# Output projection of a two-block transformer kernel: the first four row tiles accumulated together over weight chunks

## The reference

```
first block:   h = rms_norm(x) * (1 + scale) + shift          (scale, shift, gate from silu(c) @ w_ada)
               q, k, v, gates = split(h @ w_in)
               oa = forgetting_attention(...) * silu(za);  ob = sliding_window_attention(...) * silu(zb)
               y  = concat(oa, ob) @ w_out                    # 2048 x 1024 times 1024 x 1024
               x  = x + gate * rms_norm(y)
second block:  16 meta tokens ahead; a = sparse latent attention * silu(gate_a)
               r  = rms_norm(hgrn2(...)) * silu(gate_h)
               y  = concat(a, r) @ w_out
               out = layer_norm(2**0.25 * h + y) * ln_g + ln_b
```

## Time and profile before

| | |
|---|---|
| median of three runs | 3832.46 us |
| the profiled execution | 3833.1 us, span 3831.4 us |
| TensorE busy, granted clock | 3363.4 us (88%), 0.936 of 2.4 GHz |
| VectorE, ScalarE, GpSimd busy | 2068.3, 1388.9, 894.7 us |
| output stage one, first and last matmul | 1522.72 and 1699.21 us |
| output stage two, first matmul and last result | 3639.14 and 3828.25 us |
| matmuls of L850, each of three kinds | x512, 396, 393 and 393 ns mean |

### The profile page before, as it was taken

The page is one execution under the profiler, slowest core; times in us unless marked ns, Lnnn a source line. Parts: engine busy times, 40 slices in busy tenths (PEclk is TensorE's granted clock), DMA queues, the critical chain, the costliest instruction groups (busy, mean ns, idle before and its releaser), DMA issues. The chain is left out here.

```text
span 3831.4 us, 44650 instructions
## 1 busy us (share of the span) xinstructions
PE 3363.4 (88%) x15906; PEld 2532.0 (66%) x15906; DVE 2068.3 (54%) x3915; ACT 1388.9 (36%) x2368; POOL 894.7 (23%) x815
## 2 busy tenths in 40 slices
PE   6898999699999996986699989795996989999698
PEld 3688888566656664875577768584774656666387
DVE  4200101366666665331489999995674544545466
ACT  3100001034444444221258888122553333333344
POOL 0120111156454461001322222242231021111100
PEclk9899999889999998998899999897997999999899
DMA  6221223456554423444211353245135354444454
GB/s 220 63 76 51 77 76 117 125 123 130 119 122 109 106 71 109 132 148 164 71 47 54 91 182 90 84 144 172 56 116 166 104 134 122 118 112 113 129 159 130
DMA packets 386851, 433.92 MB, mean 113 GB/s; under 512 B 113046, under 2 KB 302838, under 8 KB 374824
## 3 DMA queue, kind: packets, MB, share of 16 engines
q1 hardware_dynamic: 276044, 306.45, 28.6%
q10 hardware_dynamic: 104000, 86.95, 7.8%
q0 software_dynamic: 6592, 37.75, 3.5%
HBM read 298.41 MB, written 132.62 MB: 113 GB/s over the span
## 5 line engine op out<-in xcount | busy, mean ns | idle before, releaser
L2179 PE MATMUL f_pO<-f_PT,f_vv 128*128 128x512 f32 (+3 forms) x944 | 379.3, 484 | 25.0 <-ACT f_PT L2208 25.0
L2266 DVE CUSTOM_DVE_ANT_0 n_junk<-n_pM,n_chosen 128x512 bf16<-128x512 f32 (+4 forms) x352 | 200.8, 572 | 305.1 <-PE n_pM L2100 150.4
L2261 DVE TENSOR_REDUCE f_mxc<-f_pM 128x1 f32<-128x512 f32 (+2 forms) x448 | 240.0, 540 | 222.3 <-PE f_pM L2104 127.9
L2575 PE MATMUL cbank<-hT_high,cw_hi 128*128 128x512 f32 x800 | 321.4, 402 | 35.9 <-POOL kpartsI L2547 15.9
L2754 DVE TENSOR_SCALAR_CACHE_REDUCE sharedI<-xI,TI 128x384 bf16<-128x384 f32 (+8 forms) x284 | 349.0, 1294 | 0.1
L590 PE MATMUL p_bank<-hT_high,p_w_hi 128*128 128x512 f32 (+1 forms) x768 | 306.7, 399 | 43.6 <-POOL p_w_lo L556 38.6
L2208 ACT ACTIVATE f_PT<-f_pS 128x512 f32<-128x512 f32 (+3 forms) x472 | 221.2, 473 | 334.3 <-PE f_pS L2143 165.8
L2208 ACT ACTIVATE n_PT<-n_pS 128x512 f32<-128x512 f32 (+4 forms) x352 | 177.6, 504 | 424.3 <-PE n_pS L2158 424.1
L2575 PE MATMUL cbank<-hT_high,cw_lo 128*128 128x512 f32 x800 | 316.0, 395 | 0.0
L2575 PE MATMUL cbank<-hT_low,cw_hi 128*128 128x512 f32 x800 | 315.4, 394 | 0.0
L2179 PE MATMUL n_pO<-n_PT,n_vv 128*128 128x512 f32 (+4 forms) x704 | 312.8, 526 | 0.0
(11 more groups left out here) (408 smaller groups left out, 7387.6 us busy)
## 6 DMA issues: line engine op xcount, KB each, us to landing
n_mkt<-scratch_mask_turned ACTq DMA_DIRECT2D x256, 128.0 KB, 2.1
cw_raw<-in_w_in_dram SPq DMA_DIRECT2D x50, 512.0 KB, 4.6
f_zz<-scratch_z SPq DMA_DIRECT2D x128, 128.0 KB, 3.0
p_w_raw<-in_w_in_dram SPq DMA_DIRECT2D x23, 512.0 KB, 3.9
wa<-in_w_ada_dram SPq DMA_DIRECT2D x8, 1024.0 KB, 5.8
xt<-in_x_dram SPq DMA_DIRECT2D x16, 512.0 KB, 6.8
scratch_z<-p_stage ACTq DMA_DIRECT2D x32, 256.0 KB, 2.4
scratch_qk_high<-p_stage ACTq DMA_DIRECT2D x32, 256.0 KB, 2.5
```

What stands on the lines that cost most here:

```text
L2179: pe.matmul(pO[:, B % 2, c0:c1], lhsT=vv[0:nk, b, kt, :], rhs=PT[0:nk, u % PR, c0:c1], start=(kt == 0 and not heads[h].local), stop=(heads ...
L2261: v.tensor_reduce(to, pM[:, n % 2, 0:wd], AX.X, ALU.max).then_inc(s_mx, 1)
L2266: v.tensor_tensor_reduce(junk[:, n % 2, 0:wd], pM[:, n % 2, 0:wd], chosen[:, at:at + wd], 1.0, 3.0 * NEG, ALU.add, ALU.max, accum_out=to). ...
L2575: last = pe.matmul(bank[:, p % RING, 0:wd], lhsT=w_part[pw][b][:, c, :], rhs=rhs, start=(c == 0 and a == 0), stop=(c == DC - 1 and a == 2))
```

## The change

In both output stages the first FIRST = 4 row tiles are multiplied together: for weight chunk k, TensorE does all 6 matmuls of each of the four tiles, then goes to chunk k+1. pY gets four buffers (eight banks), G_hi and G_lo four each. Tiles 4 to 15 are multiplied as before. The weights come in eight DMAs of 512 KB. The engines' order is written out anew in `in_order`, and SP's order in the loops after `load`. gT, og, zg, xg and tt keep two buffers. One more wait stands in VectorE's gate (s_lo).

```
-        AHEAD, BEHIND = 3, 1
-        def skeleton(phases): ...
+        FIRST = 4
+
+        def in_order(gate, split, finish, weight):
+            for n in range(FIRST):
+                for g in ((0, 1) if n == 0 else (n + 1,)):
+                    gate(g)
+                split(n)
+                weight(n)
+            for k in range(FIRST, DC):
+                weight(k)
+            for n in range(FIRST, NT + 2):
+                if n < NT:
+                    split(n)
+                if n + 1 < NT:
+                    gate(n + 1)
+                for t in {FIRST: (0, 1), FIRST + 1: (2, 3)}.get(n, (n - 2,)):
+                    finish(t)
```

On SP (the waits within load_parts, load_turned, load_rows and store are as before):

```
-            parts = ((3, load_parts),) if part is not None else ()
-            skeleton(parts + ((2, load_turned), (-1, store), (1, load_rows)))
+            def load(n):
+                if part is not None:
+                    load_parts(n)
+                load_turned(n)
+            for n in range(2):
+                load(n)
+            for n in range(2):
+                load_rows(n)
+            for n in range(2, 6):
+                load(n)
+            for n in range(NT):
+                store(n)
+                if n + 2 < NT:
+                    load_rows(n + 2)
+                for t in {0: (), 1: (6,), 2: (), 3: (7,)}.get(n, (n + 4,)):
+                    if t < NT:
+                        load(t)
```

On TensorE:

```
-                pe.wait_ge(s_lo, n + 1)
-                pe.wait_ge(s_res[b], r)
-            for z in range(2):
-                pe.wait_ge(s_wl[z], DC // 2)
-            skeleton(((0, multiply),))
+            for k in range(DC):
+                pe.wait_ge(s_wl[k % 2], k // 2 + 1)
+                for n in range(FIRST):
+                    if k == 0:
+                        pe.wait_ge(s_lo, n + 1)
+                    for z in range(2):
+                        last = products(n, k, z)
+                    if k == DC - 1:
+                        last.then_inc(s_y, 1)
+            for n in range(FIRST, NT):
+                pe.wait_ge(s_lo, n + 1)
+                pe.wait_ge(s_res[n % 2], n // 2 - 1)
+                for z in range(2):
+                    for k in range(DC):
+                        last = products(n, k, z)
+                last.then_inc(s_y, 1)
```

`products(n, k, z)` is the three passes of tile n, chunk k, half z, into pY[:, n % 4]. On GpSimd, ScalarE and VectorE:

```
-            for k in range(0, DC, 2):
-                gp.dma_start(wraw[:, k:k + 2, :], ...).then_inc(s_w[k // 2], 16)
-            split_low(gp, 1)
+            for k in range(DC):
+                gp.dma_start(wraw[:, k, :], w_out[0, k * P:(k + 1) * P, :]).then_inc(s_w[k], 16)
+            for k in range(1, DC, 2):
+                weight_low(gp, k)
...
-            skeleton(((1, high), (-1, finish)) + (((2, gate),) if part is not None else ()))
+            in_order(gate, high, finish, weight)          # ScalarE
...
                 if n >= 2:
                     v.wait_ge(s_hi, n - 1)
+                    v.wait_ge(s_lo, n - 1)
...
-                if n >= 2:
-                    v.wait_ge(s_y, n - 1)
+                if n >= 4:
+                    v.wait_ge(s_y, n - 3)
...
-            skeleton(((1, low), (-1, finish)) + (((2, gate),) if part is not None else ()))
+            in_order(gate, low, finish, weight)           # VectorE
```

More of the change, by code:

```diff
@@ L757, in stage_out @@
             sig = m.sb(n_("sig"), [P, HW])
-        G_hi = [m.sb(n_(f"Ghi{i}"), [P, DC, P], F32R) for i in range(2)]
-        G_lo = [m.sb(n_(f"Glo{i}"), [P, DC, P], F32R) for i in range(2)]
+        G_hi = [m.sb(n_(f"Ghi{i}"), [P, DC, P], F32R) for i in range(4)]
+        G_lo = [m.sb(n_(f"Glo{i}"), [P, DC, P], F32R) for i in range(4)]
         junk = m.sb(n_("junk"), [P, D])
@@ L764, in stage_out @@
             gain, offset = m.sb(n_("gain"), [P, D]), m.sb(n_("offset"), [P, D])
-        pY = m.ps(n_("pY"), [P, 2, D])
-        s_w = [m.sem(n_(f"w_loaded{i}")) for i in range(DC // 2)]
+        pY = m.ps(n_("pY"), [P, 4, D])
+        s_w = [m.sem(n_(f"w_loaded{i}")) for i in range(DC)]
         s_wh, s_wl = m.sem(n_("w_high")), [m.sem(n_(f"w_low{i}")) for i in range(2)]
@@ L814, in load_turned, with load_rows, store @@
                 sp.dma_start(gT[:, b], gated_T.rearrange("(k p) t -> p k t", p=P)[:, :, ds(n * P, P)]).then_inc(s_gt[b], 16)
-            def load_rows(n, b, r):
+            def load_rows(n):
+                b, r = n % 2, n // 2
                 sp.wait_ge(s_res[b], r)
                 sp.dma_start(xg[:, b, :], rows_in[ds(n * P, P), :]).then_inc(s_x[b], 16)
-            def store(n, b, r):
+            def store(n):
+                b, r = n % 2, n // 2
                 sp.wait_ge(s_res[b], r + 1)
@@ L825, in _, with weight_low @@
+            for n in range(NT):
[5 more added lines that the diff above has]
+                        load(t)
             for b in range(2):
                 sp.wait_ge(s_st[b], 8 * NT)
[L828 to L833, removed]
+        def weight_low(eng, k):
+            eng.wait_ge(s_wh, k + 1)
+            eng.tensor_tensor(w_lo[:, k, :], wraw[:, k, :], w_hi[:, k, :].bitcast(F32), ALU.subtract
+                              ).then_inc(s_wl[k % 2], 1)
@@ L843, in _, with products @@
         def _(pe):
-            def multiply(n, b, r):
+            def products(n, k, z):
+                for a, (pg, pw) in enumerate(PASSES):
+                    last = pe.matmul(pY[:, n % 4, z * HW:(z + 1) * HW], lhsT=(G_hi, G_lo)[pg][n % 4][:, k, :],
+                                     rhs=(w_hi, w_lo)[pw][:, k, z * HW:(z + 1) * HW],
+                                     start=(k == 0 and a == 0), stop=(k == DC - 1 and a == 2))
+                return last
+            for k in range(DC):
[7 more added lines that the diff above has]
+                        last.then_inc(s_y, 1)
@@ L853, in multiply, with weight, gate @@
                 last.then_inc(s_y, 1)
-            for z in range(2):
-                pe.wait_ge(s_wl[z], DC // 2)
-            skeleton(((0, multiply),))
         @block.scalar
         def _(act):
-            for k in range(DC):
-                act.wait_ge(s_w[k // 2], 16)
+            def weight(k):
+                act.wait_ge(s_w[k], 16)
                 act.activation(w_hi[:, k, :], wraw[:, k, :], ACT.Copy).then_inc(s_wh, 1)
-            def gate(n, b, r):
+            def gate(n):
+                if part is None:
+                    return
+                b, r = n % 2, n // 2
@@ L867, in gate, with high, finish @@
                 act.activation(sig[:], zg[:, b, :], ACT.Sigmoid).then_inc(s_sig, 1)
-            def high(n, b, r):
+            def high(n):
+                b, r, c = n % 2, n // 2, n % 4
                 act.wait_ge(s_gt[b], r * 16 + 16)
-                if n >= 2:
-                    act.wait_ge(s_y, n - 1)
-                last = act.activation(G_hi[b][:, 0:GIVEN], gT[:, b], ACT.Copy)
+                if n >= 4:
+                    act.wait_ge(s_y, n - 3)
+                last = act.activation(G_hi[c][:, 0:GIVEN], gT[:, b], ACT.Copy)
                 if part is not None:
                     act.wait_ge(s_gated, n + 1)
-                    last = act.activation(G_hi[b][:, GIVEN:].rearrange("p a b -> p (a b)"), g1[:, b, :], ACT.Copy)
+                    last = act.activation(G_hi[c][:, GIVEN:].rearrange("p a b -> p (a b)"), g1[:, b, :], ACT.Copy)
                 last.then_inc(s_hi, 1)
-            def finish(n, b, r):
+            def finish(n):
+                b = n % 2
                 if ln:
@@ L893, in _, with weight, gate @@
             own_ = Tally(v, s_dve)
-            split_low(v, 0)
-            def gate(n, b, r):
+            def weight(k):
+                if k % 2 == 0:
+                    weight_low(v, k)
+            def gate(n):
+                if part is None:
+                    return
+                b, r = n % 2, n // 2
                 v.wait_ge(s_in[b], r * 32 + 32)
@@ L941, in finish @@
                 else:
-                    own_.up(v.scalar_tensor_tensor(tt[:, b, :], pY[:, b, :], rstd[:, one], gate_row[:],
+                    own_.up(v.scalar_tensor_tensor(tt[:, b, :], pY[:, n % 4, :], rstd[:, one], gate_row[:],
                                                    ALU.mult, ALU.mult))
```

33 lines of the change are left out of this document (14 added, 19 removed).

## The result

| | before | after |
|---|---|---|
| median of six runs | 3832.74 us | 3901.55 us (3892.93 to 3906.14) |
| ratio after / before | | 1.0176, 95% interval 1.0161 to 1.0191 |
| profiled span | 3831.4 us | 3899.3 us |

A forecast was written before the change was run, and what follows sets the result against it. TensorE was taken to bound the first output stage and VectorE's order of work to pace the second. Stage one -5 us and stage two +61 us gave +56 us: 3889 us, range 3858 to 3906.

The forecast's parts named there:

- stage one, gain: First output stage: TensorE starts 16 us sooner, but waits leave a gain of 5 us, between 2 and 10.
- stage two, first matmul sooner: Second stage's opening: the first matmul waits for the second zg and comes at 3636.5, only 2.6 us sooner.
- stage two, end of tile 0's product: Second stage: tile 3's further rounds of loads put the end of tile 0's last matmul (E0) at 3685.5, 3677 to 3688.
- a turn of the ring: Second stage: store, load, gate, finish, next store form a closed ring, 15.6 us a tile against 11.27.
- from tile 0's product to the last result: Second stage: first finishes, nine ring rounds and the last three finishes sum to 203.6 us from E0.
- TensorE's stops for the finish of tile 0: Before tile 4, TensorE stands still about 2.3 us in the first stage and 8 us in the second.
- The clock: Second stage's ring: each tile begins at low clock, 13.4 us a tile, under 15.6, so it costs nothing.
- (a): Rival, second stage: no ring, parts land in time; second stage +17.5, total +12, 3846 us; chance 8%.
- (b): Rival, faster: first parts land by 3628, both stages start 10 to 15 us sooner, end 3825; chance 4%.
- (c): Rival, second stage: TensorE never leaves the low clock in the ring, 20.5 us a tile, 3950 us; chance 3%.
- (d): Rival: the early start is hidden wholly and the ring is as forecast; inside the main range, no separate chance.
- The change of PSUM bank: Output stages: a bank change every 3 matmuls, 64 times a stage, costs nothing; upper end 13 us.

The follow-up runs named there:

- e1: Changed kernel with the loads of tile n+4 issued ahead of the store of tile n instead of behind it; 3846.28 us, ratio 1.0026 to before.
- e2: Changed kernel with the finish of the older tile ahead of the gate of the next, SP's order as changed; 3857.94 us, ratio 1.0063 to before.
- e5: Changed kernel with xg of tile n+2 loaded behind the loads of tile n+4, all still behind the store; 3885.03 us, ratio 1.0132 to before.
- e8: e7 with one edit: loads of tile n+4 behind the store of tile n, as in the change; 3862.47 us, ratio 1.0067 to before.
- e6: Change in stage one only, stage two as before, with gT given four buffers instead of two; 3833.52 us, ratio 0.9990 to before.
- e7: Changed kernel with FIRST = 2, loads ahead of the store, gain and offset behind the parts of tiles 0 and 1; 3811.63 us, ratio 0.9929 to before.

## Why the prediction was right, and where its sizes were off

Forecast 3889 (3858 to 3906), measured 3901.55, near the upper end. The mechanism was the forecast one, and e1, e2, e5 and e8 each show it from another side. All the misses go the same way: 4.1 us in stage one, 2.8 in the opening of stage two, 6.8 behind it. Term by term, from the stage's first load:

| term | forecast | measured |
|---|---|---|
| stage one, gain | 5 | 0.9 |
| stage two, first matmul sooner | 2.6 | 2.8 |
| stage two, end of tile 0's product (before's stage start at 3611.7) | 73.8 | 76.6 |
| from there to store 0 | 11.9 | 11.8 |
| a turn of the ring | 15.6 | 16.3 (mean of ten) |
| from tile 0's product to the last result | 203.6 | 210.4 |
| TensorE's stops for the finish of tile 0 | 2.3 and 8 | 2.52 and 7.9 |

**The ring's turn.** I put the issue of zg 1.3 us behind the store with 0.37 for og, as in the earlier trace rows where og had waited for a semaphore. Issued straight behind xg, og occupies the queue 0.79 us and zg goes at 1.70. That is 0.4 of the 0.6 to 0.7. The landing, 5.1, was as the row said; gate and finish came to 9.37 (3750.20 to 3759.57) where I had 9.2. One turn was 17.3; its zg is the one of 6.18 in the chain above. The ten turns made 162.9 us where I had 156: that is the whole of the 6.8 us in the last line but one. (The ends that I gave for the ring, 44 and 74 us, were worked out for nine turns, where the sum has ten.) My sign that the sigmoid would wait about 5 us was right for VectorE's first product, 5.67, but ScalarE's own wait was 8.09, since it had been done sooner.

**Stage one.** The mis-sized term is tile 3's inputs with the rest of low clock behind them. I had tile 3 ready 22.9 us after the stage's start and 0.9 for the clock; it was ready at 25.6 (its split ends at 1517.11), the clock rose about 1519, and tile 0's product ended at 62.4 where I had 60.3. Another 1.5 us lie behind TensorE's stop of 2.52: tiles 4 to 15 took 132.1 instead of 130.6. The stretches 1557 to 1562 and 1562 to 1567 were granted 0.80 and 0.86; from 1560.42 to 1563.49 seven matmuls went at 0.44 us each instead of 0.227, which is the 1.5. I had taken a wait of 5.47 us as the sort that lowers the clock and put nothing on one of 2.5. e6 shows besides that the reason I gave for the late gT, the wait for the split, was not what set it.

**Stage two's opening.** The first matmul went as forecast: the second zg holds it. The loads and the waits of TensorE:

```profile
3611.99 5.62 SPq L818 DMA_DIRECT2D o_og<-scratch_rr  x1
...
3617.66 5.17 SPq L818 DMA_DIRECT2D o_zg<-scratch_gate_h  x1
...
3629.67 0.63 ACT L907 ACTIVATE o_sig<-o_zg 128x512 f32<-128x512 f32 x1 [2.43 <-DMA o_zg<-scratch_gate_h]
...
3633.86 0.80 PE L873 MATMUL o_pY<-o_whi,o_Ghi 128*128 128x512 f32 x1 [31.82 <-DVE o_wlo L859]
...
3637.82 0.79 PE L873 MATMUL o_pY<-o_whi,o_Ghi 128*128 128x512 f32 x1 [1.03 <-DVE o_Glo L963]
...
3642.61 0.80 PE L873 MATMUL o_pY<-o_whi,o_Ghi 128*128 128x512 f32 x1 [1.86 <-DVE o_Glo L963]
...
3648.51 0.50 PE L873 MATMUL o_pY<-o_whi,o_Ghi 128*128 128x512 f32 x1 [2.97 <-DVE o_Glo L963]
```

SP's issue is held 5.62 and 5.17 us, ScalarE's sigmoid of tile 1 starts at 3629.67, and each of the next three tiles costs a wait (1.03, 1.86, 2.97).

The start of the four products together is set by another path, the further rounds of loads for tile 3: the chain above goes from the first zg (3610.57, 16.01 us) through tile 0's gate to tile 2's zg (3628.62, 6.12 us) and on to tile 3's split, which ends at 3648.46. That is 39.2 us from the stage's first load where I had 37.3, and the low clock lasted ten matmuls from there where I had six: these make most of the 2.8 us. The landings were no later than I had put them; two instructions of VectorE on the chain were longer. The product of og and zg and the low part of tile 3 (L963, at 3645.61) took 2.66 and 2.85 us, where such instructions take 0.69 in the ring. Both times GpSimd was subtracting a weight chunk:

```profile
3637.47 2.53 POOL L859 TENSOR_TENSOR o_wlo<-o_wraw,o_whi 128x1024 fp32r<-128x1024 f32 x1 [23.46 <-ACT o_whi L899]
...
3637.90 2.66 DVE L949 TENSOR_TENSOR o_g<-o_og,o_zg 128x512 f32<-128x512 f32 x1
```

The kernel before has the same at 3633.27 (2.83 us), and e1 at 3646.10 (2.66). No run took GpSimd's part away, so the cause is not shown; my sum had no term for it.

**The clock** cost nothing in the ring, as forecast: from 3730 to 3800 there are 208 matmuls at 0.87, with TensorE idle 13.6 us in four waits, and TensorE is not on the chain there. The Trainium skill's rule (TensorE: Matmul & The Clock Gate, HAM oscillation) says that a kernel which waits for DMA between short groups of matmuls starts each group at the low clock. The trace agrees: behind each of the four waits, of 2.24 to 4.48 us, seven to ten matmuls go at 0.43 us. The ring hides it. In stage one, where TensorE is the bound, the low clock behind the stop of 2.52 us is paid.

**Rivals.** (a), no ring, was 3846, with +17.5 in stage two and -5 in stage one; e1, which has none, is at 3846.28 with +13.7 and -0.4. That the totals agree is luck: VectorE's pace without the ring is 10.47, not 11.27. (b) failed on the second zg, as its condition said; e7 shows that even with gain and offset behind the parts it lands at 18 us. (c) did not occur: the granted clock from 3730 to 3800 is 0.87. (d) is half true: in stage one the early start is hidden almost wholly.

**Not settled.** Why og and zg land so late beside the weights, and why SP's issue is held 4 to 6 us at the opening: that its queue is full is a reading, which no run tested. Nor whether e7's early start could be had without its wait of 1.15 us.

**The change of PSUM bank.** I left up to 13 us for it in the range and nothing in the sum. The trace after shows that it costs nothing. While four tiles are multiplied together, with a new bank every three matmuls:

```profile
1519.20:1557.50 38.30, 38.30 (x170) 31.72 (x169) 5.87 (x4) 4.55 (x8) 6.83 (x3) 1.00 0.04 11
```

170 in 38.30 us is 0.225 us each, and by their starts 0.227, as in the earlier trace rows with a change every 24.

## What to carry to other kernels

When an order of loads and stores is written anew, follow one buffer round: if the load of a later tile stands behind a store, and the use of that load stands ahead of the work that releases the next store, a full DMA latency joins every tile, and no single wait in the profile is long (here the landing is 5.1 us and comes back ten times). Starting an engine sooner is worth what its last-needed input allows: here 15.4 us of early start gave 0.9 us with four tiles, and 16.0 gave 13.6 with two, whose inputs are loaded before anything else. A consumer that runs all groups to their end together also hands them on together; leave free banks behind the group, so that the next tile does not wait for the first finish (e7).

## What the runs showed of the hardware that was not expected

SP's issue of og took 0.37 us as the first after a wait and 0.43 straight behind the store (e5), but 0.79 behind store and xg; that is where the 1.70 in the ring comes from. The place in the run does not explain it, since behind gain and offset at the stage's opening og took 0.43 as well (3610.10). A load issued 3.6 us earlier, while the DMA engines moved 393 to 401 GB/s, landed at the same moment (e6). TensorE's clock was granted 0.80 and 0.86 in the stretches with and behind an idle time of only 2.52 us. An instruction of VectorE with two inputs took 2.66 us instead of 0.69 while GpSimd worked on one of its own.
